# Rows turned by split loads and VectorE instead of TensorE, in the mixing stage and in the expert steps

## What is computed

```python
h = rms_norm(x, g_mix)
a_in, a_gate, u, v = split(h @ w_in)                  # 4 x 512 columns
a, hist = conformer_conv(a_in, a_gate, ...)           # a_in * sigmoid(a_gate), causal conv of 31 taps, LayerNorm, silu
b = u * (tril(w_sg) @ layer_norm(v) + b_sg)           # in chunks of 128 tokens
x = x + concat(a, b) @ w_out
x = x + memory_attend(rms_norm(x, g_xattn), mem_k, mem_v, w_xq, w_xo)   # 4 heads, 256 memory tokens
h = rms_norm(x, g_ffn)
# top 1 of 4 groups, then top 2 of its 8 experts for each token
x = x + sum_k gate_k * (silu(h @ w_eg[e_k]) * (h @ w_eu[e_k])) @ w_ed[e_k]
y = rms_norm(x, g_final)
```

## Time and profile before

| | |
|---|---|
| time, median of 3 runs | 2449.04 us (2448.23 to 2449.22) |
| the profiled execution | 2448.84 us, its span 2447.1 us |
| TensorE busy | 2385.7 us, 97% |
| VectorE busy | 1015.4 us, 41% |
| GpSimd, ScalarE busy | 559.4 us, 447.8 us |
| DMA | 427.32 MB, 175 GB/s on average |
| mixing, prompt attention, samples, router, experts | 852, 85, 56, 523, 916 us |

### The profile page before, as it was taken

One profiled execution on the slowest core, in us unless ns is written; L12 is line 12 of the kernel. 1 busy time (PEld: TensorE's weight loads), 2 busy tenths in 40 slices (PEclk: granted clock), 3 DMA queues, 4 the chain that ended last, 5 costly groups with the idle time before them and its releaser, 6 DMA issues.

```text
span 2447.1 us, 33019 instructions
## 1 busy us (share of the span) xinstructions
PE 2385.7 (97%) x10639; PEld 1162.2 (47%) x10640; DVE 1015.4 (41%) x2549; ACT 447.8 (18%) x1012; POOL 559.4 (23%) x711
## 2 busy tenths in 40 slices
PE   8999999999999998999999998999999999999998
PEld 4444444444444484444444443444444444444443
DVE  1585665666679022355555543222222222222222
ACT  2222212212211123111111111111111111111111
POOL 1122232132133000001111113233233323333231
PEclk9999999999999999999999999999999999999999
DMA  6302111111132334665444427967597749797994
GB/s 239 108 30 68 39 37 62 39 47 53 40 116 108 139 144 163 204 195 132 130 125 129 112 90 274 339 213 276 176 361 269 252 174 365 264 351 268 351 355 148
DMA packets 186899, 427.32 MB, mean 175 GB/s; under 512 B 27875, under 2 KB 51963, under 8 KB 186667
## 3 DMA queue, kind: packets, MB, share of 16 engines
q1 hardware_dynamic: 155810, 351.41, 42.2%
q0 software_dynamic: 30656, 74.14, 8.3%
q10 hardware_dynamic: 336, 0.54, 0.1%
HBM read 351.89 MB, written 88.52 MB: 180 GB/s over the span
## 4 chain that ended last, share of the span: by engine, by line
PE 57%; DMA 1%; DVE 1%; issue 0%; POOL 0%; ACT 0%; POOLq 0%; SPq 0%; DVEq 0%; ACTq 0%
PE r_pss L2216 17%; PE r_psx L2216 12%; PE r_psx L2175 10%; PE r_pss L2155 8%; PE r_psk L2216 6%; PE r_pst L2205 2%; PE r_psr L2187 1%; PE r_psr L2225 1%; PE r_pss L2225 0%; PE r_pss L2217 0%; DMA table_scratch<-r_val,r_slot 0%; PE r_pss L2261 0%; DMA r_x1n<-h_scratch,e_token 0%; PE r_psx L2217 0%; PE r_psk L2217 0%
## 5 line engine op out<-in xcount | busy, mean ns | idle before, releaser
L790 PE MATMUL a_psz<-W 128*128 128x512 f32 x1088 | 479.4, 594 | 0.1
L2216 PE MATMUL r_pss<-W,r_h2T 128*64 x1312 | 431.3, 487 | 3.3 <-issue 3.3
L2217 PE MATMUL r_pss<-W,r_h2T 128*64 128x256 f32 (+1 forms) x1312 | 431.3, 487 | 0.0
L628 DVE SCALAR_TENSOR_TENSOR yacc<-aext,pcol,yacc 128x256 f32<-128x256 f32 x928 | 370.9, 479 | 0.0
L790 PEld LDWEIGHTS a_psz<-W 128*128 128x128 f32 x1088 | 203.0, 191 | 235.2 <-issue 234.7
L2216 PEld LDWEIGHTS r_pss<-W,r_h2T 128*64 128x64 f32 x1312 | 180.0, 137 | 256.2 <-issue 214.9
L2217 PE MATMUL r_psx<-W,r_x1r 128*64 128x512 f32 x656 | 290.3, 595 | 0.0
L2216 PE MATMUL r_psx<-W,r_x1r 128*64 x656 | 290.3, 595 | 0.0
L2175 PE MATMUL r_psx<-W 128*128 128x512 f32 x544 | 239.1, 597 | 3.6 <-PEq L123 2.4
L2155 PE MATMUL r_pss<-W,r_h2T 128*128 128x512 f32 x480 | 209.8, 595 | 0.0
L2217 PEld LDWEIGHTS r_pss<-W,r_h2T 128*64 128x64 f32 x1312 | 180.0, 137 | 0.0
(11 more groups left out here) (360 smaller groups left out, 2643.4 us busy)
## 6 DMA issues: line engine op xcount, KB each, us to landing
W<-in_w_expert_gate SPq DMA_DIRECT2D x32, 2048.0 KB, 12.0
W<-in_w_expert_up SPq DMA_DIRECT2D x32, 2048.0 KB
W<-in_w_expert_down SPq DMA_DIRECT2D x32, 2048.0 KB
W<-in_x_prompt SPq DMA_DIRECT2D x32, 512.0 KB, 4.2
x_scratch<-W SPq DMA_DIRECT2D x18, 512.0 KB, 3.0
r_x1r<-x_scratch SPq DMA_DIRECT2D x17, 512.0 KB, 4.4
x_scratch<-r_x SPq DMA_DIRECT2D x17, 512.0 KB, 5.3
h_scratch<-r_h SPq DMA_DIRECT2D x17, 512.0 KB, 2.6
```

Source lines behind the costliest of these rows:

```text
L628: ins = dve.scalar_tensor_tensor(out=out, in0=src, scalar=w, in1=yacc[:, i, :], op0=ALU.mult, op1=ALU.add)
L790: last = pe.matmul(psz[bank][:], hT[t.par][:, k, :], w_in[bank][:, k, :], start=(k == 0), stop=(k == KD - 1))
L2216: pe.matmul(out[0:HALF, :], xt[:, 0:HALF], W[:, bass.ds(base + at, n)], start=start, stop=stop)
L2217: return pe.matmul(out[HALF:P, :], xt[:, HALF:P], W[:, at:at + n], start=start, stop=stop)
```

## The change

- **Mixing, x.** From tile 2 on, the normalised x goes from SBUF to DRAM (`xn_scratch`), comes back in four pieces, and DVE turns it into hT (128x1024). ACT then multiplies hT in place by the gain, 8 instructions: before u's copy up to step 3, behind it from step 4. PE's `turn_x` stays for tiles 0 and 1.
- **Mixing, b.** b is stored as it is, loaded in four pieces, and turned by DVE (128x512). PE's turn and ACT's copy go; the turn of the normalised y waits for the copy of the one before it instead.
- **Mixing, a.** a of the 16 prompt tiles goes to DRAM, comes back in four pieces and is turned by DVE in the next step. The sample tile is still turned by PE.
- The columns of hT, a and b now stand in another order, and so do the rows of w_in and w_out (two loads) and the small constants.
- The convolution of the samples is cut in 14 taps (step 18) and 17 taps (step 19, after b's turn). The turn of the keys in step 20 stands behind the output product.
- **Sample stage.** The 16 score products of the router are issued in parts of 2, 2, 6, 1, 1 and 4.
- **Expert weights.** Gate and up parts are loaded with 8 neighbouring rows of the matrix on a partition (16 KB in one run instead of 8 runs of 2 KB). The down part of the third slot is loaded after the first gather has landed.
- **Experts.** For all steps but step 1, rows are gathered by four indirect DMAs of 128 pieces of 1 KB, and DVE turns them (128x1024) behind its copy of the hidden units; 16 small DVE instructions make the piece numbers. Step 1 keeps one gather, PE's turn and the two copies. ACT's copy of the lower half of the turned hidden units is cut in two, and the down products start with its two blocks. The turn of expert tile 0 in the router is DVE's.

```diff
 # SP, mixing
+def split_x(t):
+    sp.wait_ge(S["normed"], t.v + 1)
+    need(sp, S["x_turned"], t.v - TURNED)
+    sp.dma_start(xn_d, xn[:]).then_inc(S["xn_out"], 16)
+    sp.wait_ge(S["xn_out"], 16 * (t.v - TURNED + 1))
+    load_split(sp, xs, xn_d, S["xs_here"])
+def split_a(t):
+    sp.wait_ge(S["a_done"], t.v + 1)
+    need(sp, S["stage_full"], t.v)
+    sp.dma_start(a_d, a_tok[t.par][:]).then_inc(S["a_out"], 16)
+    sp.wait_ge(S["a_out"], 16 * (t.v + 1))
+    load_split(sp, as_, a_d, S["as_here"], DC)
...
 # SP's step
                         if s.at(-3).exists():
                             load_b(s.at(-3))
+                        if s.at(1).exists() and s.v + 1 >= TURNED:
+                            split_x(s.at(1))
...
                         if s.at(-1).exists():
                             store_b(s.at(-1))
+                        if s.exists(PT):
+                            split_a(s)
 # ACT, mixing
+def gain_hT(t):
+    act.wait_ge(S["x_turned"], t.v - TURNED + 1)
+    for k in range(KD):
+        last = act.activation(hT[t.par][:, k, :], hT[t.par][:, k, :], ACT.Copy, scale=gm[:, k:k + 1])
+    last.then_inc(S["hT_done"], 2)
...
 # DVE's step in mixing: a behind the y statistics; b and x behind the v statistics
+                            turn_split(dve, aext[t.half % 2][:, :, HIST + P * t.par:HIST + P * t.par + P], as_).then_inc(S["stage_full"], 1)
...
-                            conv_sample()
+                            conv_sample(range(0, 14))
...
+                            turn_split(dve, mbl[t.par], bs).then_inc(S["b_turned"], 1)
+                        if static and s.v == PT + 3:
+                            conv_sample(range(14, TAPS))
...
+                            turn_split(dve, hT[x.par], xs).then_inc(S["x_turned"], 1)
 # PE's step in mixing
-                        if s.at(1).exists():
+                        if s.v + 1 < TURNED:
                             turn_x(s.at(1), 0)
...
-                            for c in range(CG):
-                                last = pe.transpose(psx[:, c, :], b_tok[:, P * c:P * c + P], ident[:])
-                            last.then_inc(S["bT_psum"], 1)
...
 # expert weights
-                          I[name][0][bass.ds(e, 1), :, :].rearrange("a (k p) n -> p (a k) n", p=P)).then_inc(here, 16)
+                          I[name][0][bass.ds(e, 1), :, :].rearrange("a (k p) n -> p (a k) n" if n == 2 else "a (p k) n -> p (a k) n", p=P)).then_inc(here, 16)
 # POOL, experts
+                        for b in range(QUADS):
+                            c = D // QUADS
+                            pool.indirect_dma_start(out=xg[t.par][:, c * b:c * b + c], out_offset=None,
+                                                    in_=h3_rows.rearrange("t (q c) -> (t q) c", q=QUADS),
+                                                    in_offset=bass.IndirectOffsetOnAxis(ap=token[t.par][:, b:b + 1], axis=0)).then_inc(x_here[t.par], 16)
 # DVE, experts
-                        dve.tensor_copy(xT[t.par][:, 4:8, :], pst[:, 4:8, :]).then_inc(T["xT_done"], 1)
+                        turn_split(dve, xT[t.par][:], xg[t.par][:]).then_inc(T["xT_done"], 1)
 # PE, experts
                         turn_h(t, 0)
-                        if j < LAST - 1:
-                            turn_x(t.at(1), (0, 1, 2, 3))
-                            turn_x(t.at(1), (4, 5, 6, 7))
                         turn_h(t, 1)
```

284 lines of the change are left out of this document (160 added, 124 removed).

## The result

The changed kernel takes 2392.34 us (median of 4 runs, 2391.52 to 2394.14), the kernel before 2448.64 on the same chip (4 runs, 2444.7 to 2449.22): ratio 0.9774, 95% interval 0.9757 to 0.9791. The profiled execution took 2391.94, with a span of 2390.2; against the 2448.84 of before that is 56.9 us, where the sum of the terms was 67.0. The forecast of 2382 was 10 us too low; the time lies inside its range.

A forecast was written before the change was run, and what follows sets the result against it. The prediction took TensorE to bound the kernel, busy 2385.7 us of a span of 2447.1. Its terms summed to 67.0 us, taken from 2448.84, forecasting 2382 us; own range 2373 to 2400, with rivals B and C 2370 to 2416.

The forecast's parts named there:

- Steady mixing: Mixing steps 4 to 16: fewer TensorE turns cut the period from 45.25 to 43.0 us; 27.0 us saved, bounds 22 to 28.5.
- Early steps: Mixing steps 0 to 3: gain 4 us together, bounds 1 and 6, with up to 1 us of stall in steps 1 to 3.
- Tail: Mixing steps 17 to 20: split sample convolution, turns removed and keys' turn moved save 8.9 us, bounds 6 and 10.
- Sample stage: Sample stage: the router's 16 score products, dealt out into TensorE's gaps, save 3 us, bounds 1 and 5.
- Router and handoff: Router loses eight transposes, 0.9 us; at the handoff the first gather's wait shrinks by 2 us, bounds 0 and 3.
- Experts: Expert loop: seam from last up to first down product falls from 1.77 to 1.22 us; 21.2 saved, bounds 18.4 and 22.4.
- Rival A: Expert loop: small gathers behind long weight runs delay scatter landing, GpSimd's 2.3 us room runs out; 2478 us, chance 0.10.
- Rival B: Mixing: VectorE's additional turns starve GpSimd's x1 add, so the mixing gain of 27 is gone; 2409 us, chance 0.15.
- Rival C: Expert seam gives nothing: VectorE comes later to the hidden product, seam stays 1.77, 21 us lost; 2403 us, chance 0.12.

The follow-up runs named there:

- run 6: Changed kernel with three issue orders changed: tile 3's gain row before VectorE's tap run at step 2, x_attn turns before token adds, gm load before gx: 2432.96 us.
- run 7: Changed kernel with three parts undone: sample convolution in one piece, score products in two eights, third slot's down part loaded early: 2448.1 us, one run.
- run 3: Changed kernel with six more small GpSimd instructions and a wait for their end behind the gathers of each expert step: 2478.4 us.
- run 10: Kernel of run 9 with TURNED = 3 instead of 2, so TensorE also turns the x rows of tile 2: 2386.51 us.
- run 8: Changed kernel with ScalarE's copy of the low half of hT in one piece instead of two: 2433.0 us.
- run 11: Kernel of run 8 with GpSimd's four gathers in the loop started behind both turns of h: 2398.24 us.
- run 2: Changed kernel with the experts' gate and up parts loaded in eight runs of 2 KB per partition again: 2442.74 us.
- run 1: Changed kernel with expert rows gathered by one DMA from step 2 on and turned by TensorE between its turns of h, as before: 2409.13 us.
- run 4: Changed kernel with the first expert turn of h before the last three pairs of up products, the second behind the first pair of down products: 2434.24 us.
- run 12: Changed kernel with one more wait on VectorE at mixing step 2, for a value reached long before: 2431.77 us, one run.
- run 5: Kernel of run 4 with GpSimd waiting for both turns of h before it issues the four gathers: 2389.36 us.
- run 9: Kernel of run 5 with the handoff and gm orders of run 6, and without the late gather in the last four steps: 2389.96 us.

## Why the prediction was right, and where it was off

**Steady mixing (27.0; 27.9).** Right in mechanism and size: 42.97 us a step where 43.0 was worked out, no wait of the yn turn, and VectorE's turns at 1.10 and 2.00 us.

**Early steps (4; -1.0).** The step that failed is "in steps 1 to 3 up to 1 us of stall in each". There was one stall, of 3.5 us at the end of step 3, with a block at half clock behind it (10.01 for 7.03), and 1.15 us more at the start, where the first matmul begins at 9.47 instead of 8.32. The forecast compared chains of DMAs with the length of a step and took VectorE's sum over a steady stretch for room. In the pipe's filling steps of 28 us VectorE has none, and run 6 shows that its order, not the chain, is what is late. Step 4 shows it as well: it took 45.5 us before (136.61 to 182.13), takes 45.95 now and 45.5 in the two kernels with full clock in it, where a steady step is 42.97.

**Tail (8.9; 6.9).** The split of the convolution gave what was said of it: run 7 puts it at 5.4, forecast 5.7. The turn of the keys behind the output product shows as a wait of 2.32 instead of 3.81 us at the next stage, 1.5 where 1.3 was forecast. The rest is short by the new wait of 1.4 for VectorE's ybuf, behind its longer turns, and one of 0.6.

**Sample stage (3; 1.0).** The mechanism and nearly the size were right, and the clock hides it. TensorE's idle time in the stage fell from 9.9 to 7.3 us, 2.5 of the 3; its busy time rose from 46.8 to 48.4 with the same matmuls, at a mean clock of 0.97 for 1.00. Runs 3, 6 and 10, which split the products as here and have full clock, take 54.1 to 54.2 us for the stage, run 7 with the two eights 56.7. The wait for the second scores is filled; what is short of 3 goes with a wait of 2.0 us for the cached values, which was 0.3. Whether the split brings the clock fall on isn't shown: it stood at the start of the router before and in run 7, and here in the sample stage, but in three kernels with the split in neither.

**Router and handoff (2.9; 5.2).** That it came out above the forecast is the clock's doing, luck for the sum: 3.1 us in the router, by the windows above. Of the change are the 0.9 of the transposes and 1.2 at the handoff. The wait for the gather fell by 3.0, from 5.8 to 2.8, the upper bound; in run 7, where the down part loads early again, the handoff is 2.6 us longer. A new wait of 2.8, for VectorE's copy behind sixteen token adds, took part of it: these adds were costed at 2.4 us in the loop, where they are covered, and not at the handoff, where they are not (timeline of VectorE):

```profile
1473.06 2.52 DVE L2027 TENSOR_SCALAR e_token<-e_pair 32x1 int32<-32x1 f32 x16 [2.51 <-DMA e_pair<-table_scratch]
1475.61 0.69 DVE L2035 COPY r_h2T<-r_pst 128x512 f32<-128x512 f32 x1
```

**Experts (21.2; 15.5).** The seam was forecast at 1.22 and is 1.32 to 1.40. That halving the copy is worth 0.1 is borne out by runs 8 and 11 (21.90 for 21.79); what takes it back against the 1.31 of the earlier trace rows is not known. One step more, the one in which TensorE leaves the loop, takes 26.01 us: a wait of 2.30 with no releaser, and a clock of 0.72 over the six us behind it. Before, the same wait stood in a step of 24.78 at full clock, with 22.25 around it. That is 1.6 us of the miss, and nothing of it was forecast.

**Rival A** didn't occur. Gathers of 1 KB rows beside weight rows of 16 KB wait no longer for the scatter: 102.7 us in 23 waits, up to 5.4, against the earlier trace rows. A gate part lands in 8.7 us, where it took 12.0. With 2 KB rows (run 2, whose steps are longer by the late seams) the waits are 109.3 in 26. By the rule of the Trainium skill that was named beside this rival, long packets would hold the small ones up; no run here shows it. The rival's arithmetic was sound, though: run 3 puts GpSimd's room at 2.3 us.

**Rival B** came true in one place, the stall at 137 us, and cost nothing in the steady steps. GpSimd's sigma was held up for 9.33 us by VectorE's run. The rule of the Trainium skill ("SBUF — State Buffer", SBUF: two separate sides) agrees: the run has two SBUF operands, and what it holds up here is a GpSimd instruction with only one. But run 6 shows that lifting this alone gains nothing.

**Rival C** is excluded by run 1: the seam gives 16.8 us.

**What the forecast did not have.** Six kernels that differ from the changed one by a small edit (runs 2, 4, 6, 7, 8, 12) lost 40 to 50 us, two thirds or more of the whole gain, at the place that rival C named: VectorE comes late to the hidden product. From 28 to 34 us of it is idle time of TensorE; the rest is longer busy time with the same products, in all but run 4 from the clock. Shown is that it goes with the issue of GpSimd's pair loads in the two us behind the turn (the table above), and that moving gathers and pair loads behind the seam ends it (run 11 against 8, run 5 against 4, and on one and the same chip run 5 against 6, 7 and 8, and runs 9, 10 and 11 against 12). Open is why the changed kernel, with 14 such seams, has none that is late. Every kernel of the experiments with the loads in that place has the delay, on all three chips, and the changed kernel was not run beside them. So two explanations stand: something that any edit shifts (where code or queues lie; run 2 has as many instructions as the changed kernel and other descriptors, run 12 the same descriptors and one wait more), or the chip and the time. Running the changed kernel beside run 12 would have told them apart. That the pair loads alone are enough rests on the sorting of seams and on run 3; moving them alone, without the gathers, was not tried. The 2392 of the changed kernel is true of its four runs; I would not promise it for the next build or another chip.

## What to carry to other kernels

Room on an engine, as a sum over a steady stretch, says nothing of the filling steps of a pipe and of handoffs: go through the engine's own order there, instruction by instruction, before a turn or sixteen small adds are put on it. Keep runs of GpSimd's DMA issues away from the moments at which a short chain between TensorE, VectorE and ScalarE is released: one wait on GpSimd did it here and gave 2389.4 us with even steps of 21.68. And when a small edit gives a large change in a part that it doesn't touch, try an edit that does nothing before explaining it, and run the unedited kernel beside it on the same chip, which was not done here. Before a difference of one or two us in a stage is put down to an edit, take TensorE's busy and idle time and the granted clock of the stage: here the clock hid 1.6 us of one term and lent 3.1 to another.

## What the runs showed of the hardware

- Starts of VectorE and ScalarE on finished TensorE work were held back, mostly 1.6 to 3.0 us and together, where GpSimd issues small loads behind indirect gathers, in six kernels, and not in the changed one with the same timing (1.77 against 0.12 us), which ran apart from them.
- Behind an idle time of TensorE of 3.5 us the granted clock was 0.50 in the changed kernel and 1.00 in runs 8 and 10; behind the same 2.32 us at the start of the q stage sixteen turns took 1.94, 3.03 and 3.56 us in three kernels.
- A gate part of 2 MB landed in 8.7 us in rows of 16 KB (changed kernel) and in 12.0 in rows of 2 KB (kernel before), with other traffic changed as well.
- The q stage took 84.40 us in every kernel with a granted clock of 1.00 in it, and 85.3 to 86.2 in those with a stretch at 0.50.
- An issue of GpSimd behind six small GpSimd operations of 3.15 us waited 1.5 us more.
